# A decoder step with gathered experts: 24 tokens by row where it was 16, thinner gate maps, a third probability buffer, and half of the scaling on GpSimd

## The reference

```python
q = (xb @ w_pq).reshape(TOKEN_BLOCK, PEER_HEADS, PEER_DKEY)
s1, s2 = q[..., :half] @ sub_k1.T, q[..., half:] @ sub_k2.T      # per head
v1, i1 = lax.top_k(s1, 16); v2, i2 = lax.top_k(s2, 16)
best, pos = lax.top_k(v1[..., :, None] + v2[..., None, :], 16)   # over 256 sums
gate = softmax(best)
act = gelu(einsum('td,thkd->thk', xb, expert_u[eidx]))
out = einsum('thk,thkd->td', gate * act, expert_v[eidx])
```

## Time and profile before

| what | value |
|---|---|
| median of 3 runs | 2310.1 us (2305.84 to 2310.73) |
| profiled execution, its time | 2311.11 us |
| its span, first to last instruction | 2309.2 us |
| mean granted TensorE clock | 0.984 |
| busy: PE, PEld, DVE, ACT, POOL | 96%, 87%, 51%, 13%, 17% |
| DMA moved | 843.21 MB, mean 365 GB/s |

### The profile page before, as it was taken

One profiled execution on the slowest core, in us unless ns is written; L12 is line 12 of the kernel. 1 busy time (PEld: TensorE's weight loads), 2 busy tenths in 40 slices (PEclk: granted clock), 3 DMA queues, 4 the chain that ended last, 5 costly groups with the idle time before them and its releaser, 6 DMA issues.

```text
span 2309.2 us, 35404 instructions
## 1 busy us (share of the span) xinstructions
PE 2207.9 (96%) x14282; PEld 2015.7 (87%) x14282; DVE 1179.1 (51%) x2095; ACT 301.2 (13%) x926; POOL 386.3 (17%) x414
## 2 busy tenths in 40 slices
PE   7999998789889879999999999999999999999998
PEld 5677776577589868999999999899999999999998
DVE  3200003833566647767777544599744444444422
ACT  2000001722221012011111110144200000000000
POOL 0100000022302011232212221133311111111100
PEclk9999999999999989999999999999999999999999
DMA  7999982289959898999999999999999999999974
GB/s 280 405 413 381 385 316 81 80 333 357 398 201 396 345 383 315 407 398 422 422 421 420 420 420 420 372 372 376 402 422 421 422 422 421 422 422 422 421 315 155
DMA packets 117787, 843.21 MB, mean 365 GB/s; under 512 B 14432, under 2 KB 16608, under 8 KB 30656
## 3 DMA queue, kind: packets, MB, share of 16 engines
q1 hardware_dynamic: 62752, 485.30, 52.4%
q0 software_dynamic: 54128, 354.58, 37.7%
q10 hardware_dynamic: 816, 2.11, 0.2%
HBM read 834.25 MB, written 74.78 MB: 394 GB/s over the span
## 4 chain that ended last, share of the span: by engine, by line
PE 64%; DMA 23%; DVE 8%; issue 2%; ACT 1%; POOL 1%; SPq 0%; DVEq 0%; POOLq 0%; ACTq 0%
PE low L1414 39%; PE big L1414 24%; DMA BIG<-expert_u,VB 20%; DVE BIG L1240 4%; DMA WR<-wall 1%; DMA BIG<-kaT 1%; ACT BIG L630 1%; DMA BIG<-expert_v,VB 1%; DMA BIG<-memT 0%; DMA BIG<-va 0%; DVE CST L968 0%; POOL BIG L525 0%; DVE BIG L846 0%; PE low L1538 0%; DVE HT L883 0%
## 5 line engine op out<-in xcount | busy, mean ns | idle before, releaser
L1414 PE MATMUL low<-HT,WR 128*128 128x176 f32 (+3 forms) x6336 | 1081.9, 333 | 8.4 <-DMA WR<-wall 7.0
L1414 PEld LDWEIGHTS low<-HT,WR 128*128 128x128 f32 x6336 | 984.2, 191 | 98.2 <-issue 9.7
L1414 PE MATMUL big<-BIG,WR 128*128 (+3 forms) x2888 | 450.7, 312 | 11.3 <-DVE XT L891 7.1
L1253 DVE SCALAR_TENSOR_TENSOR XT<-BIG,VB,XT 128x2048 f32<-128x2048 f32 x128 | 300.9, 2351 | 302.7 <-DMA BIG<-expert_v,VB 302.4
L1414 PE MATMUL low<-BIG,WR 128*128 (+3 forms) x2616 | 434.8, 321 | 12.6 <-DMA WR<-wall 10.3
L1414 PEld LDWEIGHTS big<-BIG,WR 128*128 128x128 f32 x2888 | 419.3, 193 | 30.1 <-issue 18.5
L1240 DVE SCALAR_TENSOR_TENSOR BIG<-BIG 128x2048 f32<-128x2048 f32 x144 | 329.5, 2291 | 210.8 <-DMA BIG<-expert_u,VB 209.7
L1414 PEld LDWEIGHTS low<-BIG,WR 128*128 128x128 f32 x2616 | 411.0, 192 | 17.8 <-issue 10.5
L539 POOL DMA_INDIRECT BIG<-expert_u,VB x144 | 161.5, 1122 | 683.8 <-DVE BIG L1240 609.5
L545 POOL DMA_INDIRECT BIG<-expert_v,VB x144 | 161.5, 1122 | 558.2 <-DVE XT L1253 477.3
L914 DVE TENSOR_SCALAR BIG<-low 128x320 f32 x32 | 15.7, 492 | 264.0 <-PE low L1414 264.0
(11 more groups left out here) (230 smaller groups left out, 1124.0 us busy)
## 6 DMA issues: line engine op xcount, KB each, us to landing
WR<-uT SPq DMA_DIRECT2D x128, 1024.0 KB
WR<-expert_v SPq DMA_DIRECT2D x128, 1024.0 KB
WR<-wall SPq DMA_DIRECT2D x122, 1024.0 KB
BIG<-va POOLq DMA_DIRECT2D x48, 512.0 KB, 11.0
BIG<-kaT POOLq DMA_DIRECT2D x64, 384.0 KB, 11.0
BIG<-kmT SPq DMA_DIRECT2D x2, 2048.0 KB, 12.9
BIG<-vm SPq DMA_DIRECT2D x8, 512.0 KB, 13.4
XT<-xT SPq DMA_DIRECT2D x1, 2560.0 KB, 21.9
```

What stands on the lines that cost most here:

```text
L1253: nc.vector.scalar_tensor_tensor(out=x_tok, in0=rows_of(row), scalar=weight, in1=x_tok, op0=ALU.mult, op1=ALU.add).then_inc(s_vsum, 1)
L1414: return nc.tensor.matmul(out, lhsT, rhs, start=start, stop=stop, skip_group_check=True)
```

## The change

Five edits at once:

- `FEWER`: 8 more of the 192 tokens are taken out of the dense part. 8 tokens x 8 heads x 2 halves of the 16 choices fill 128 partitions, so they are 8 further rows in each pass (152 rows), and `DENSE` is 168. Their tokens are repeated over the partitions by a DVE copy, turned by PE and copied by ACT (`turn_fewer`) at chunks 98 to 101, in the buffer of the first tokens' rows, which by then is free.
- The 42 maps are made during chunks 80 to 121, one per chunk, in three PSUM banks instead of four. The turn of the choices (`TURN`) moves from chunk 92 to 72, the gates' exponentials from 64 to 56, the issue of the choices from 80 to 64. 108 rows are done ahead (`ROWS_BEFORE`), the rest beside the maps, 5 per 4 chunks; choosing takes two parts each five rows.
- Prompt attention has a third probability buffer, in the place of queries already used; the inverse of the sums is taken as before, the maxima of pair p go ahead of the scaling of pair p - 1, and the second head's scaling is GpSimd's.
- In sample attention and cross-attention, additions to the stream go ahead of the next request's softmax, and the tiles of the cross output projection use three banks from tile 6 on.
- SP loads the memory keys and values of the first four requests three chunks later, and half of the second four requests' values with them, into other places, after a wait for the choices of group 2.

```diff
-FEW = 16
+FEW, FEWER = 16, 8
+ALONE = FEW + FEWER
-DENSE = REST - FEW
+DENSE = REST - ALONE
-EXPS, TAIL = 64, 80
-TURN = 92
-MAP_LO, MAP_HI = 100, 124
+EXPS, TAIL = 56, 64
+TURN = 72
+MAP_LO, MAP_HI = 80, 122
+E2_AT = 98
-ROWS = SLOTS + FEW
+ROWS = SLOTS + FEW + FEWER
+V_FEW = (*range(SLOTS, SLOTS + FEW), *range(40), *range(SLOTS + FEW, ROWS), *range(40, SLOTS))
-ROWS_BEFORE = 141
+ROWS_WEIGH = 98
+ROWS_BEFORE = 108
-    return 2 if c % 3 == 0 else 1
+    return 2 if c % 4 == 0 else 1
-FEW_OUT = 96
+FEW_OUT, FEWER_OUT = 32, 96
...
-                if before == POS["out", 1, 15]:
+                if before == POS["cq", 1, 0]:
                     sp.wait_ge(s_used, FREED["out", 1, 15])
                     mem_keys(0)
-                    mem_values(0)
+                    mem_values(0, 0, 4)
+                    sp.wait_ge(s_sc, 3)
+                    sp.wait_ge(s_idx, 3)
+                    mem_values(1, 0, 2)
...
+            for p in range(HEADS):
+                wide, narrow = probs_p(p)
+                rd = stat[:, 16 * (p % 2) + 14:16 * (p % 2) + 16]
+                pool.wait_ge(s_rden, p + 1)
+                nc.gpsimd.tensor_scalar(wide[:, 1], wide[:, 1], rd[:, 0:1], None, ALU.mult)
+                nc.gpsimd.tensor_scalar(narrow[:, 1], narrow[:, 1], rd[:, 1:2], None, ALU.mult).then_inc(s_nrm2, 1)
...
+                act.dma_start(chosen[FEW * h:FEW * (h + 1), :, SLOTS:SLOTS + FEW], few_src[:, :, h * PK:(h + 1) * PK]).then_inc(s_few, 16)
+                for half in range(2):
+                    to, k = half * 64 + h * FEWER, h * PK + half * FEWER
+                    act.dma_start(chosen[to:to + FEWER, :, SLOTS + FEW:ROWS], fewer_src[:, :, k:k + FEWER]).then_inc(s_few, 16)
...
-                    if p >= 2:
-                        dve.wait_ge(s_T, 2 * p - 2)
+                    if pair_in_buffer(p) >= 0:
+                        dve.wait_ge(s_T, 2 * pair_in_buffer(p) + 2)
...
-                if last:
-                    dve.wait_ge(s_dv, mr)
-                    nc.vector.tensor_scalar(pl[:, 0, 0:256], pl[:, 0, 0:256], rd[:, 0:1], None, ALU.mult)
-                    nc.vector.tensor_scalar(pl[:, 0, 256:384], pl[:, 0, 256:384], rd[:, 1:2], None, ALU.mult).then_inc(s_nrm, 1)
...
                 if last:
-                    nc.vector.tensor_scalar(pl[:, 1, 0:256], pl[:, 1, 0:256], rd[:, 2:3], None, ALU.mult)
-                    nc.vector.tensor_scalar(pl[:, 1, 256:384], pl[:, 1, 256:384], rd[:, 3:4], None, ALU.mult).then_inc(s_nrm, 1)
+                    dve.wait_ge(s_rden, p)
+                    nc.vector.tensor_scalar(wide_l[:, 0], wide_l[:, 0], rd[:, 0:1], None, ALU.mult)
+                    nc.vector.tensor_scalar(narrow_l[:, 0], narrow_l[:, 0], rd[:, 1:2], None, ALU.mult).then_inc(s_nrm, 1)
...
-                if n + 1 < REQ:
-                    softmax_s(n + 1)
-                for f in (*with_scores, *with_turn):
+                for f in with_scores:
                     add_to_stream(FIRST_TILE, CROSS, f)
...
+                if n + 1 < REQ:
+                    softmax_s(n + 1)
+                for f in with_turn:
+                    add_to_stream(FIRST_TILE, CROSS, f)
...
-                if n % 3 == 0 and later:
+                if (n - ROWS_AHEAD) % 5 in (0, 2) and later:
...
-                if g >= 4:
-                    pe.wait_ge(s_gcp, g - 3)
+                if g >= 3:
+                    pe.wait_ge(s_gcp, g - 2)
...
+            def turn_fewer(part):
+
+                pe.wait_ge(s_rep, 2)
+                if part:
+                    pe.wait_ge(s_fewer_h, part)
+                for k in range(4):
+                    at = (4 * part + k) * P
+                    ins = nc.tensor.transpose(bank[7][:, k * P:(k + 1) * P], h_tok[:, at:at + P], ident)
+                ins.then_inc(s_fewer_t, 1)
...
+            v_chunks(MAP_LO, FEWER_OUT)
+            pe.wait_ge(s_vsum, FEWER_AT + FEWER)
+            for k in range(KT):
+                mm(v_all[k][:, FEW:ALONE], h_few[:, k * P:(k + 1) * P], pick_fewer, start=False, stop=True)
+            v_chunks(FEWER_OUT, NCH - WR_N)
```

More of the change, by code:

```diff
@@ L167, in build @@
         HT = region("HT", KT * NT)
-        BIG = region("BIG", NCH * DENSE + (URING + 2) * D)
+        BIG = region("BIG", ROOM + (URING + 2) * D)
         OT = BIG[:, 0:KT * NT]
@@ L223, in build @@
         VTF = QK[:, T_VA * NT:T_IN * NT]
-        probs_p = VTF[:, 0:1536].rearrange("p (b s c) -> p b s c", b=2, s=2)
+        probs_two = VTF[:, 0:1536].rearrange("p (b s c) -> p b s c", b=2, s=2)
+        q_pairs = [QK[:, (T_QA + 2 * i) * NT:(T_QA + 2 * i + 2) * NT].rearrange("p (s t) -> p s t", s=2) for i in range(2)]
         probsT_p = VTF[:, 1536:2304].rearrange("p (s c) -> p s c", s=2)
@@ L257, in build @@
         C_by = C.rearrange("p (c t) -> p c t", t=DENSE)
-        h_few = BIG[:, NCH * DENSE:NCH * DENSE + D]
-        u_ring = [BIG[:, NCH * DENSE + (1 + r) * D:NCH * DENSE + (2 + r) * D] for r in range(URING)]
-        h_tok = BIG[:, NCH * DENSE + (URING + 1) * D:NCH * DENSE + (URING + 2) * D]
+        h_few = BIG[:, ROOM:ROOM + D]
+        u_ring = [BIG[:, ROOM + (1 + r) * D:ROOM + (2 + r) * D] for r in range(URING)]
+        h_tok = BIG[:, ROOM + (URING + 1) * D:ROOM + (URING + 2) * D]
         v_ring = u_ring + [h_tok]
@@ L305, in tile_out @@
             if g == FIRST_TILE:
-                at = f % 2 if stage == "pq" else 5 + f % 2
+                at = f % 2 if stage == "pq" else (5, 6, 0)[(f - 6) % 3] if stage == "co" and f >= 6 else 5 + f % 2
             else:
@@ L810, in _ @@
                 nc.scalar.activation(late[:, 0:m], u[:, 0:m], ACT.Gelu).then_inc(s_dev, 1)
+                if E2_AT <= c < E2_AT + 4:
+                    part = c - E2_AT
+                    act.wait_ge(s_fewer_t, part + 1)
+                    nc.scalar.activation(h_tok[:, part * 512:(part + 1) * 512], bank[7], ACT.Copy).then_inc(s_fewer_h, 1)
                 if c == DOTS_DONE:
@@ L1339, in _ @@
             dve.wait_ge(s_turn, 1)
-            dve.wait_ge(s_few, 16 * PH)
-            own = P - FEW
+            dve.wait_ge(s_few, 16 * 3 * PH)
+            own = P - ALONE
             for z in range(3):
-                nc.vector.tensor_copy(turned[z][:, 0:own], bank[6][:, z * P + FEW:(z + 1) * P])
+                nc.vector.tensor_copy(turned[z][:, 0:own], bank[6][:, z * P + ALONE:(z + 1) * P])
                 nc.vector.tensor_copy(turned[z][0:64, own:DENSE], bank[7][0:64, z * 64:(z + 1) * 64])
@@ L1906, in dense_v @@
                         pe.wait_ge(s_dev, NCH - UB + k // 2 + 1)
-                    ins = mm(v_all[k][:, FEW:REST], WR[:, slot_of(r) * D + k * P:slot_of(r) * D + (k + 1) * P], coefs, start=(first and k % 2 == 0), stop=last)
+                    ins = mm(v_all[k][:, ALONE:REST], WR[:, slot_of(r) * D + k * P:slot_of(r) * D + (k + 1) * P], coefs, start=(first and k % 2 == 0), stop=last)
                     if last:
```

123 lines of the change are left out of this document (80 added, 43 removed).

## The result

| what | before | after |
|---|---|---|
| median of the runs | 2310.07 us (2305.84 to 2310.73) | 2326.80 us (2326.29 to 2327.98) |
| span of the profiled execution | 2309.2 us | 2324.9 us |
| busy: PE, PEld, DVE, ACT, POOL | 96%, 87%, 51%, 13%, 17% | 94%, 85%, 52%, 13%, 18% |
| DMA moved | 843.21 MB | 860.10 MB |

A forecast was written before the change was run, and what follows sets the result against it. The second half was taken as a DMA budget, 2.485 us per unit, PE 4% behind. Terms -7 (prompt attention) - 5 - 1.5 - 1 + 11 (experts) = -3.5 gave 2306 us, range 2281 to 2328.

The forecast's parts named there:

- Last row at about +1296: Expert passes: last gathered row done 1296 us after the end of expert chunk 0, from 507 units of 2.485 us plus idle.
- 24 + 6 + 5: Idle DMA in us: 24 in the row gap ahead of chunk 80, 6 at the u-to-v hand-over, 5 at the end.
- DMA bounds this stage too, and the 23 us of idle DMA go: Map stage, chunks 80 to 121: DMA sets its pace, and the 23 us idle there before vanish.
- Map stage 5.59 us a chunk: Map stage: 2.25 DMA units make 5.59 us per chunk, against 5.47 for PE and 5.1 for the DVE.
- the map stage holds rows back: Rival, chance 0.22: DVE, ACT and PE in a ring around each map; at 6.1 us a chunk 21 us more, 2328.
- Prompt attention 7 us: Prompt attention: 0.45 us of scaling moves behind the maxima in each of 16 steps, winning 7 us.
- the sign of being wrong that the prediction named: Prompt attention: the second head's transposes wait for GpSimd.
- The rival (2337): Rival, chance 0.06, prompt attention: GpSimd's pair of multiplies takes 3 us, costing 24 us instead of giving 7.
- Sample attention, third bank, memory loads 7.5 us: Sample and cross-attention: additions before the softmax win 5 us, third bank 1.5, moved memory loads 1.
- More is won: Rival, chance 0.30: slower u rows close the gap ahead of chunk 80, idle DMA 20 us, attention gives 20: 2283.
- PE sets the pace: Rival, chance 0.07, expert chunks: the whole 54.6 us of thinner matmuls is won, 2241.
- The tail: After the last row: 22 us to the program's end, 18.2 plus 3 to 4 for PE's lower clock.

The follow-up runs named there:

- experiment 4: Changed kernel with 120 rows instead of 108 ahead of the map stage and the eight tokens turned at chunks 90 to 93: 2298.19 us, 0.9944 to the kernel before.
- experiment 2: Kernel before with the prompt attention edits alone (third buffer, order of maxima and scaling, second head on GpSimd): 1.0011 to the kernel before.
- experiment 1: Kernel before with all edits ahead of the experts, expert stages unchanged: 2298.92 us, 0.9950.
- experiment 5: Changed kernel without its 16 extra gathers and their products, dense matmuls still 168 columns, eight tokens' expert part missing: 2292.58 us, 0.9923 to the kernel before.
- experiment 7: Second head's scaling on the DVE instead of GpSimd: in experiment 1's kernel 0.9924, in experiment 6's last kernel 0.9871, both to the kernel before.
- experiment 3: Kernel before with the edits in sample and cross-attention and the moved memory loads alone: 0.9950 to the kernel before.
- experiment 6: Kernel of experiment 1 with expert_v gathers in two buffers (1.0196), tied to PE's chunks (2293.28 us), or tied from earlier on (2282.27 us, 0.9876).

## Why the prediction was wrong, point by point

The mechanism was right: the second half is a DMA budget, 16 gathers cost it 40 us, rows end last, and the time behind chunk 0 goes up. What failed is the sum. It said -14.5 us ahead of chunk 0 and +11 behind it; it was -10.9 and +26.6. The time measured, 2326.8, lies inside the stated range only because a rival at 2328 had stretched it; the forecast went the other way.

- **"Last row at about +1296": it was +1312.5, and this is the step that failed.** Its idle DMA was to be 24 + 6 + 5 = 35; it was 48. The row gap and its restart were 28 (the 24 counted only the gap), hand-over and map stage 9 against 6, the end 9 against 5. The claim "DMA bounds this stage too, and the 23 us of idle DMA go" was half true: of them some 10 stayed. The last 2 are the first pass, which ran at 419 GB/s and not 422, much as it did in the earlier trace rows. The rest is work: 509 units, not 507, one of them because chunk 0 ended 11 us earlier and the rows had not come along (47 done, 48 in the earlier trace rows). But for the gap itself, all terms of this sum that missed, missed to the same side.
- **Map stage 5.59 us a chunk:** 5.81. That is the point from which I let the rival "the map stage holds rows back" decide, and its 2328 is nearly the time measured. But experiment 4 shows the same pace, 5.74, in a kernel that is 28.6 us faster, so the number was met by luck, by another road. What the stage lost to my 5.59 is 0.22 x 42 = 9 us, and PE's stalls in it are as much:

```profile
1477.87 0.63 PE L1959 MATMUL big<-CST,BIG 128*128 128x128 f32 x4 [4.17 <-ACT BIG L855]
...
1584.41 1.27 PE L1474 MATMUL big<-HT 128*128 128x128 f32 x8 [0.64 <-ACT HT L834]
...
1594.46 1.65 PE L1474 MATMUL big<-HT 128*128 128x128 f32 x8 [4.21 <-ACT HT L834]
```

The first is the turn of the eight tokens. The others are the rival's ring of DVE, ACT and PE, in small, at the hand-over: the DVE waits for rows of expert_v, 5.88 us at 1581.34 and 2.61 at 1590.33, and makes the one-hots behind them late. Without them a chunk takes 5.60. The idle gap ahead of the stage, which stood in my own sum, was the larger part.
- **Prompt attention 7 us:** nothing in the time. The DVE's steps went from 3.98 to 3.73 us in the second half and from 3.63 to 3.29 in the first, and its last maxima came 3.0 us earlier (0.55 of that was there at the start). In the second half ACT is busy for all but 0.55 us of a step, and those it spends waiting for the maxima: the step cannot get much shorter. I had taken 0.45 off the DVE's chain without asking what ACT leaves room for. What was won is not in the time of experiment 2, and the profiles show where it goes. Busy time behind the last maxima, in the kernel before and in experiments 2, 1, 5 and 7 (on the DVE):

```profile
453.00:472.00 19.00, 14.02 (x123) 9.98 (x123) 10.40 (x38) 11.18 (x35) 2.43 (x5) 0.91 0.35 131
```

```profile
453.00:472.00 19.00, 15.18 (x116) 11.15 (x116) 7.21 (x27) 8.51 (x24) 5.40 (x8) 0.73 0.33 124
```

```profile
453.00:472.00 19.00, 16.01 (x105) 12.10 (x105) 5.92 (x22) 7.50 (x20) 4.50 (x8) 0.64 0.35 130
```

```profile
453.00:472.00 19.00, 14.26 (x134) 10.51 (x134) 10.15 (x37) 9.11 (x26) 7.54 (x12) 1.00 0.44 157
```

```profile
453.00:472.00 19.00, 15.08 (x142) 11.61 (x142) 11.22 (x44) 8.28 (x24) 4.23 (x8) 1.00 0.47 177
```

From the last maxima to PE's first long run of output tiles (471.93 before) it takes 15.9, 18.9, 20.3, 15.9 and 15.6 us. In experiments 2 and 1 the last maxima came 2.8 and 4.4 us earlier than before, and at the low granted clock PE then took 3.0 and 4.4 us longer: nothing was left. The key loads on which PE then waits are released by PE itself, so they come later too. Why one profile has the low clock (0.50, the 1.2 GHz level, from 456 to 465 in experiment 2) and another with the same edits has not, no run shows, and how often it comes in the executions that were only timed is not known. The rule of the Trainium skill that I weighed against the move ("GPSIMD Engine Reference", "Key points": elementwise work is about twice as fast on VectorE) was on the right side, and mild: GpSimd's pair took 1.60 us, the DVE's 0.63. It was late by a hair: PE's weight loads wait for GpSimd 13 times, 2.4 us in all, never more than 0.2, which is the sign of being wrong that the prediction named, at a size that costs little. The rival (2337) did not come.
- **Sample attention, third bank, memory loads 7.5 us:** 10 to 11 in experiments 1 and 3, where DMA's share had seemed to leave room for 10. All waits for the additions of the length of the earlier trace rows went; the longest left of this kind is 2.23 us at 648.72.
- **"More is won" (2283)** assumed that the gap closes; it stood open for 64 us at 270 GB/s. **"PE sets the pace" (2241)** assumed that thinner matmuls make chunks come faster; they come every 4.97. The Trainium skill's rule that stood beside it ("Trainium Kernel Development and Optimization", "Best Practices", distance by LDWEIGHTS busy) ranks the kernels of experiment 6 rightly (PEld 100% of the last stage in the faster one, 97% in the slower), but does not say what bounds them: by it the changed kernel, at 534.28 of 572 us, had 7% of PE's weight-load time to win, and the DMA that would have had to feed it was at 422 GB/s already.
- **The tail** was 21.2 us for my 22, **ACT's 24 small DMAs** held it for 17.7 us (costed at 15.8, with 18.2 to hide in) and no wait of PE shows for it, and no wait of PE for a free bank shows among those of the map stage. **The turn's stall** moved to the DVE, which waits 21.9 us at 1327.56 and has no row to take.

The 26.6 us behind chunk 0 are then: the last row 92.7 us later (29 more units of DMA, 509 for (1219.8 - 27) / 2.485 = 480, 16 of them the gathers and the others chunks that had been loaded after the last row, and 21 us more of idle DMA), and 66.1 us less behind it, as PE's tail of chunks alone is gone (87.3 before, 21.2 now). Filling the gap gives 29 back and makes the five edits together as fast as the three ahead of the experts alone. The eight tokens by row gain nothing in any form tried. What does is to hold the gathers back in the stage where PE ends last: 2282.3 and 2279.5 us, 1.2 to 1.3% below the kernel before.

## What to carry to other kernels

Where two streams share a saturated DMA, neither engine's own speed shows: making one engine's work thinner bought little here, and moving it to the other stream cost DMA bytes one for one. Ask which of the two streams may be late, and issue that one by the other's progress; in experiment 6 the bandwidth freed went to the one that ended last. And a stage's start is a cost of its own: rows made to wait for a stage leave the DMA idle before it and again while their ring refills, so have the independent work run on up to the first instruction that needs the stage.

## What the runs showed of the hardware that was not expected

Some instructions of the DVE are recorded longer beside GpSimd's elementwise work. The same 128-column scaling on the DVE, in the profile by line of prompt attention, in experiment 1 with GpSimd's pair running (first) and in experiment 7 without (second):

```profile
L1021 DVE TENSOR_SCALAR BIG<-BIG,CST 128x128 f32<-128x128 f32 x16 | 6.6, 412 | 0.0
L1020 DVE TENSOR_SCALAR BIG<-BIG,CST 128x256 f32<-128x256 f32 x16 | 5.5, 342 | 0.0
...
L542 POOL TENSOR_SCALAR BIG<-BIG,CST 128x256 f32<-128x256 f32 x16 | 16.1, 1004 | 61.2 <-DVE CST L1006 61.2
L543 POOL TENSOR_SCALAR BIG<-BIG,CST 128x128 f32<-128x128 f32 x16 | 9.6, 599 | 0.0
```

```profile
L1015 DVE TENSOR_SCALAR BIG<-BIG,CST 128x256 f32<-128x256 f32 x16 | 5.6, 347 | 0.0
L1016 DVE TENSOR_SCALAR BIG<-BIG,CST 128x128 f32<-128x128 f32 x16 | 4.5, 280 | 0.0
```

412 ns against 280, while the 256-column form beside it does not change. It costs little: in both kernels the next instruction starts 0.20 us after this one. What does come later is the scaling behind the small 128x4 instruction ahead of it (243 ns against 164): it starts 0.17 us after that one and not 0.08, and the step is 0.08 us longer. The Trainium skill ("GPSIMD Engine Reference", "Key points") says that the two share their SBUF interfaces; these rows agree with it for two forms and not for the third. GpSimd itself took 1004 ns for 256 columns and 599 for 128, about three and two times the DVE's recorded durations.

With two gathers in flight instead of four the DMA moved 393 GB/s instead of 422 in the last stage: two of 1 MB did not fill it beside the stream, three did in the first pass (419).

The granted clock of the same stretch of the same code differed between profiled executions, 0.64 to 1.00 over 453 to 472 us, and moved PE by up to 4 us.
